# Filler projections of a hybrid encoder layer: split float32r products, streamed rows, all 17 tiles in the delta-net stage

## The chip, the cores and the metric

The kernel runs on one core of one Trainium2 chip. The metric is the device time of one execution in microseconds (us). All data is float32. Some matmul operands are of type float32r, a reduced form of float32 that TensorE takes in a single instruction, where a float32 product of this kernel appears in the trace as two.

## The reference, cut to what matters

One layer of a streaming encoder over 2048 prompt rows, 16 meta rows and 32 sample rows of width 1024. Every row is normed and projected, three groups of heads mix the rows, and the gated result is projected back:

```
u = rmsnorm(h, g_pre) @ W_in          # split into q/k/v of A, B, C, decay inputs, and the gate z
o_A = sliding-window attention with sinks(q_a, k_a, v_a)      # 8 heads, 2 kv heads
o_B = stick-breaking attention(q_b, k_b, v_b)                 # 4 heads
o_C = gated delta net(conv + silu of q/k/v, decay, beta)      # 4 heads, chunks of 64
y = h + rmsnorm((o_A | o_B | o_C) * silu(z) @ W_out, g_post)
```

The outputs are y, the keys and values of A and B, and the conv and delta-net states of C.

## The kernel before, in words

The rows are laid out as T = 2176 columns in 17 tiles of 128 (48 columns of padding, 16 meta rows, 2048 prompt rows, 32 sample rows, padding), and in five blocks `BLOCKS` of 512, 512, 512, 512 and 128 columns. The kernel is a chain of six stages. Each is a block in which every engine has its own program, written out by hand in order, and the engines meet by semaphores alone; a stage ends when all engines are done. SP issues nearly all DMA transfers, in program order.

- `norm_and_transpose` (from L137). Each tile of x is loaded, normed (ACT, DVE), turned by TensorE (L283) and kept in `hT`, a resident buffer of 8 x T columns (L235). The row projections (values and decay inputs) are three products of operands split in two: high part `h_hi` by ACT (L211), low part `h_lo` by DVE (L245), then high x high, high x low, low x high (L294, 392 columns).
- `conv_and_gates`. Six channel tiles as float32 products from `hT` (L463), the conv, SiLU, norms.
- `delta_net` (from L631). Iterations m = 0 to 17. Iteration m inverts a triangle for tile m in five levels and runs the state update for tile m - 1. The products are small (64 columns) and each waits for DVE, ACT or POOL, so TensorE is given filler work between them: 17 projection tiles (5 pairs and singles for q/k, stored to `uT`; 8 gate tiles z, stored to `sz`), of which this stage holds 13. `SideProjection` (L307 to L376) does them. A unit is one tile by one block; a unit has 8 pieces, one for each 128 rows of W_in. `products` (L323) issues pieces, `keep` (L338, on ACT) copies a unit from `side_acc` to `side_stage`, SP stores it (L370) and loads the weights of the tile after next (L361). The hand-made order is `POINTS` (L679): 29 pieces in each iteration, at 13 points (`beside`, L862).
- `window_attention`. No fillers.
- `stick_breaking` (from L1329). 92 steps over the query tiles and up to 512 keys each. In a step TensorE makes scores for two heads (L1491), ACT two sigmoids (L1565, L1568), DVE two scans, one for each head (L1628), with a weight copy between them (L1648), POOL one product (L1606), TensorE transposes (L1508) and the product with the values (L1522). The last four gate tiles are fillers here, two pieces a step, none in the last 12 steps. They are gated to silu(z) by ACT and DVE (L346, L351). When the last filler is done, SP may load `w_out` into `hT` (L1462), paced by the key copies of the last 12 steps.
- `output`. Per tile, load mixed heads, gates and x; sigmoid and multiply for the first `RAWZ` = 4 gate tiles (ACT L1751, POOL L1820); gate all (DVE L1789); split (L1756, L1793); 48 products of 512 columns (L1740); norm, add, store.

The fillers are float32 products, straight from the resident rows:

```
POINTS = [4, 4] + [2, 2] * 5 + [1]                                                  # L679
t, b = divmod(n, NBLK)                                                              # L326
last = pe.matmul(self.acc[:, n % self.banks, 0:width], wslot[:, t % 2, k, :],
                 hT[:, k, c0:c0 + width], start=(k == 0), stop=(k == KT - 1))       # L333
if s < N: side.products(pe, side_piece(s), side_piece(s + 1) - side_piece(s))       # L1551
```

Of the kernel before, what the change touches and what calls it, by code (L numbers as in the profile page):

```python
# [16 lines left out]
F32 = mybir.dt.float32  # L17
# [6 lines left out]
P = 128  # L24
D = 1024
# [23 lines left out]
RAWZ = 4  # L49
# [43 lines left out]
def stream_layer(nc, io):  # L93
    top = ExitStack()
    with top:
# [19 lines left out]
        hT = sb("hT", [P, KT, T])  # L115
# [3 lines left out]
        wslot = sb("wslot", [P, 2, KT, P], st=mixers)  # L119

        mix, uT, sz = io["mix"], io["uT"], io["sz"]
# [4 lines left out]
        w_in = io["w_in"][0].rearrange("(k p) n -> p k n", p=P)  # L126

# [9 lines left out]
        def norm_and_transpose():  # L137
# [4 lines left out]
            with ExitStack() as st:  # L142
# [6 lines left out]
                h_hi, h_lo = (sb(n, [P, 2, KT, P], F32R, st=st) for n in ("h_hi", "h_lo"))  # L149
# [7 lines left out]
                x_in = [sem(f"x_in{i}", st) for i in range(3)]  # L157
                sq_done, ln_done, rstd_done = (sem(n, st) for n in ("sq_done", "ln_done", "rstd_done"))
                scaled, turned, kept = (sem(n, st) for n in ("scaled", "turned", "kept"))
                xp = io["x_prompt"][0]  # L160
                tile_of = lambda n: (0, LAST)[n] if n < 2 else n - 1
                with nc.Block() as block:
                    @block.sync
                    def _(sp):
# [12 lines left out]
                        for n in range(3, 5):  # L177
                            sp.wait_ge(turned, n - 2)
                            sp.dma_start(xin[:, n % 3, :], xp[CH + P * (n - 2):CH + P * (n - 1), :]).then_inc(x_in[n % 3], 32)
                        with sp.Fori(0, (TILES - 5) // 3) as i:  # L180
                            for u in range(3):
                                sp.wait_ge(turned, 3 * i + (u + 3))
                                sp.dma_start(xin[:, (u + 2) % 3, :],
                                             xp[bass.ds(i * (3 * P) + (CH + P * (u + 3)), P), :]).then_inc(x_in[(u + 2) % 3], 32)
                        sp.dma_start(masks, io["cb"]).then_inc(masks_in, 16)
                        sp.dma_start(cf[:, C_TRI:C_EPS], io["cf"][:, C_TRI:C_EPS]).then_inc(masks_in, 16)

                    @block.gpsimd
                    def _(pool):
                        pool.memset(xin[0:CH, 0, :], 0.0).then_inc(zeroed, 1)  # L190
                        pool.memset(xin[SP0 + NSAMP:P, 1, :], 0.0).then_inc(zeroed, 1)

                    @block.scalar
                    def _(act):
# [12 lines left out]
                        def split_high(n):  # L207
                            act.wait_ge(kept, 2 * (n + 1))
                            if n >= 2:
                                act.wait_ge(row_ready, n - 1)  # L210
                            act.activation(h_hi[:, n % 2], hT[:, :, tile_of(n) * P:(tile_of(n) + 1) * P], ACT.Copy).then_inc(high, 1)  # L211
# [15 lines left out]
                    def _(dve):  # L227
# [4 lines left out]
                        def keep(n, slot, cols):  # L232
                            dve.wait_ge(turned, n + 1)
                            for k in (0, KT // 2):
                                dve.tensor_tensor(hT[:, k:k + KT // 2, cols], tp[:, slot, k:k + KT // 2, :],  # L235
# [7 lines left out]
                        def split_low(n):  # L243
                            dve.wait_ge(high, n + 1)
                            dve.tensor_tensor(h_lo[:, n % 2], hT[:, :, tile_of(n) * P:(tile_of(n) + 1) * P], h_hi[:, n % 2].bitcast(F32),  # L245
                                              ALU.subtract).then_inc(low, 1)
# [30 lines left out]
                    def _(pe):  # L277
# [8 lines left out]
                        def row(n):  # L286
                            pe.wait_ge(low, n + 1)
                            if n >= 2:
                                pe.wait_ge(row_kept, n - 1)
                            for k in range(KT):  # L290
                                if n == 0 and k % (KT // 2) == 0:
                                    pe.wait_ge(wv_low, 1 + k // (KT // 2))
                                for p, (h_, w_) in enumerate(((h_hi, wv_hi), (h_hi, wv_lo), (h_lo, wv_hi))):
                                    last = pe.matmul(acc[:, n % 2, 0:RV], h_[:, n % 2, k, :], w_[:, k // 4, k % 4, :],  # L294
# [12 lines left out]
        class SideProjection:  # L307
# [3 lines left out]


            def __init__(self, st, kind, tiles, banks=2):
                self.kind, self.tiles, self.banks = kind, tiles, banks
                self.units = NBLK * len(tiles)
                self.pieces = KT * self.units
                self.stage = sb("side_stage", [P, 2, 512], st=st)
                self.acc = pb("side_acc", [P, banks, 512], st)
# [1585 lines left out]
```

## Time and profile before

| | |
|---|---|
| three runs | 1812.44, 1813.41, 1820.65 us, median 1813.41 |
| profiled execution | 1818.64 us, span of its instructions 1817.0 us |
| mean granted TensorE clock | 0.957 of full speed |
| busy | TensorE 1664.2 us (92%), DVE 893.9, ACT 660.2, POOL 411.8 |
| DMA | 120893 packets, 108.11 MB, 59 GB/s over the span |

Engines: PE is TensorE's matmul, PEld its weight load (which can overlap a matmul), DVE VectorE, ACT ScalarE, POOL GpSimd, SP the queue that issues most DMA transfers. A row of the timeline has its start, its duration (of the union, if it merges several), engine, line, operation, output<-inputs, shape and count, and in brackets the idle time before it with what ended it. Matmul ends are modelled, so the pitch from start to start tells more than a duration. A row of busy time by stretch has the stretch (us from the span's start), its length, the busy us and (x instructions) of PE, PEld, DVE, ACT and POOL, the granted clock, the DMA engines' share and GB/s. The stages begin at about 0, 112, 348, 960, 1162 and 1590 us of the span.

### The profile page before, as it was taken

The page shows a single profiled execution, that of the slowest core. Times are in us where ns is not written, and L with a number is a line of the kernel's source. Part 1 is how long each engine was busy: PE and PEld are TensorE (multiplying, and loading weights), DVE is VectorE, ACT ScalarE, POOL GpSimd, SP SyncE. Part 2 cuts the span into 40 slices and gives each one's busy share as a digit, 9 for nine tenths or more (in the row PEclk, how much of TensorE's full clock was granted, in tenths as well). Part 3 has the DMA queues.
Part 4 walks back from the last instruction along what each step waited for, and adds up shares of the span by engine and source line. Part 5 has one row for each costly group of instructions (what it writes and reads, how often), then busy time and mean ns, then how long its engine had stood idle before and what let it go on. Part 6 is the DMA issues. An engine that isn't in the chain of part 4 may idle for free. (4 is left out here: it accounts for less than half of the span.)

```text
span 1817.0 us, 27973 instructions
## 1 busy us (share of the span) xinstructions
PE 1664.2 (92%) x11144; PEld 998.9 (55%) x11144; DVE 893.9 (49%) x1662; ACT 660.2 (36%) x1321; POOL 411.8 (23%) x344
## 2 busy tenths in 40 slices
PE   5989998299999999999998999799999998769996
PEld 5964444155555555555554555445555555557775
DVE  5724333123333333333334777478687778843332
ACT  4522536011111111111113444345454455456654
POOL 0002321111211211211200000034333434424443
PEclk8999999599999999999996999899999999879998
DMA  4310011411111211112101111100210001466661
GB/s 134 117 26 23 12 63 0 25 37 38 37 38 37 66 38 65 49 37 63 47 31 59 34 60 47 38 30 20 76 32 18 20 18 36 125 172 179 190 182 60
DMA packets 120893, 108.11 MB, mean 59 GB/s; under 512 B 34336, under 2 KB 96064, under 8 KB 120768
## 3 DMA queue, kind: packets, MB, share of 16 engines
q1 hardware_dynamic: 117616, 95.46, 19.2%
q0 software_dynamic: 3152, 10.91, 1.6%
q8 instruction: 87, 1.43, 0.3%
q14 instruction: 38, 0.31, 0.1%
HBM read 65.37 MB, written 41.08 MB: 59 GB/s over the span
## 5 line engine op out<-in xcount | busy, mean ns | idle before, releaser
L333 PE MATMUL side_acc<-hT,wslot 128*128 128x512 f32 (+1 forms) x1360 | 572.8, 550 | 10.1 <-DVE side_stage L351 6.4
L333 PEld LDWEIGHTS side_acc<-hT,wslot 128*128 128x128 f32 x1360 | 223.7, 191 | 178.9 <-issue 155.2
L1628 DVE TENSOR_TENSOR_SCAN prod<-keepb,prod 128x512 f32<-128x512 f32 (+4 forms) x184 | 270.9, 1473 | 86.5 <-ACT keepb L1565 84.1
L1606 POOL TENSOR_TENSOR reg<-reg,prod 128x1024 f32<-128x1024 f32 (+4 forms) x92 | 158.0, 1717 | 465.9 <-DVE prod L1628 465.9
L463 PE MATMUL acc<-hT,wslot 128*128 128x512 f32 (+1 forms) x480 | 180.7, 533 | 5.3 <-DMA wslot<-in_w_in 5.3
L1565 ACT ACTIVATE keepb<-b_z 128x1024 f32<-128x1024 f32 (+4 forms) x92 | 82.0, 891 | 197.2 <-PE b_z L1496 129.2
L463 PEld LDWEIGHTS acc<-hT,wslot 128*128 128x128 f32 x480 | 84.7, 192 | 98.5 <-issue 92.9
L977 DVE COPY yh<-b_two 128x256 f32<-128x256 f32 x85 | 36.1, 424 | 190.9 <-PE b_two L794 190.9
L1740 PE MATMUL b_y<-whi,mhi 128*128 128x512 f32 x272 | 108.3, 398 | 23.1 <-DVE mlo L1793 23.1
L907 ACT ACTIVATE xh<-b_dr 128x256 f32<-128x256 f32 x85 | 32.6, 383 | 211.3 <-PE b_dr L786 211.1
L1740 PE MATMUL b_y<-wlo,mhi 128*128 128x512 f32 x272 | 107.6, 395 | 0.0
L1740 PE MATMUL b_y<-whi,mlo 128*128 128x512 f32 x272 | 107.5, 395 | 0.0
L1508 PE MATMUL b_w<-cf,reg 128*128 128x128 f32 (+1 forms) x624 | 90.0, 278 | 18.2 <-DVE wt L1648 15.0
L728 POOL TENSOR_TENSOR atl<-at,cf 128x256 f32<-128x256 f32 x102 | 72.5, 748 | 126.1 <-DVE at L958 126.1
L1522 PEld LDWEIGHTS b_o<-wt,vrow 128*64 128x64 f32 x1232 | 67.4, 139 | 53.5 <-ACT wt L1583 31.9
L1491 PE MATMUL b_z<-reg 64*128 64x512 f32 (+3 forms) x360 | 90.7, 581 | 4.8 <-PEq L1852 4.8
L733 POOL TENSOR_TENSOR osq<-oo,ors 128x256 f32<-128x256 f32 x17 | 10.4, 613 | 368.9 <-ACT ors L938 368.9
L1508 PEld LDWEIGHTS b_w<-cf,reg 128*128 128x128 f32 (+1 forms) x624 | 66.2, 141 | 47.9 <-DVE wt L1648 19.7
L344 ACT ACTIVATE side_stage<-side_acc 128x512 f32<-128x512 f32 (+1 forms) x65 | 34.6, 532 | 158.9 <-PE side_acc L333 158.9
L1522 PE MATMUL b_o<-wt,vrow 128*64 128x128 f32 x1232 | 89.5, 284 | 2.1 <-DVE reg L1635 2.0
L1568 ACT ACTIVATE reg<-b_z 128x1024 f32<-128x1024 f32 (+4 forms) x92 | 81.3, 884 | 0.0
L1828 POOL TENSOR_TENSOR yy<-yy,xres 128x1024 f32<-128x1024 f32 (+2 forms) x17 | 54.0, 3177 | 106.8 <-DVE yy L1797 94.1
(200 smaller groups left out, 2477.1 us busy)
## 6 DMA issues: line engine op xcount, KB each, us to landing
uT_scratch<-side_stage SPq DMA_DIRECT2D x36, 256.0 KB, 2.0
hT<-mix_scratch SPq DMA_DIRECT2D x17, 512.0 KB, 6.9
hT<-sz_scratch SPq DMA_DIRECT2D x17, 512.0 KB, 8.1
sz_scratch<-side_stage SPq DMA_DIRECT2D x32, 256.0 KB, 2.0
reg<-in_x_prompt SPq DMA_DIRECT2D x15, 512.0 KB
wslot<-in_w_in SPq DMA_DIRECT2D x15, 512.0 KB, 3.9
xres<-in_x_prompt SPq DMA_DIRECT2D x15, 512.0 KB
out_y_prompt<-yy POOLq DMA_DIRECT2D x15, 512.0 KB, 6.4
```

The source lines that it names most:

```text
L333: last = pe.matmul(self.acc[:, n % self.banks, 0:width], wslot[:, t % 2, k, :], hT[:, k, c0:c0 + width], start=(k == 0), stop=(k == KT - 1))
L463: last = pe.matmul(acc[:, b, 0:w], wslot[:, c % 2, k, :], hT[:, k, c0:c0 + w], start=(k == 0), stop=(k == KT - 1))
L728: pool.tensor_tensor(atl[:, l], at[:, :, :], wide(lvl(l), 4), ALU.mult).then_inc(level, 1)
L1491: last = pe.matmul(b_z[0:R, s % 2, hh, 0:nk], reg[half, QS + a, q0:q0 + R], reg[half, KS + a, k0:k0 + nk], start=True, stop=not masks, ski ...
L1508: last = pe.transpose(b_w[0:kn, hh, t, 0:R], beta[0:R, s % 3, hh, at:at + kn], ident[0:R, 0:R])
L1522: last = pe.matmul(b_o[hh * CH:hh * CH + CH, 0:R], v, wt[part, s % 2, hh, t, 0:R], start=(first and t == 0), stop=(last_ and t == len(head ...
L1565: act.activation(keepb[0:R, s % 2, :, 0:nk], b_z[0:R, s % 2, :, 0:nk], ACT.Sigmoid, scale=-SCALE).then_inc(keep_ready, 1)
L1568: act.activation(beta[0:R, s % 3, :, 0:nk], b_z[0:R, s % 2, :, 0:nk], ACT.Sigmoid, scale=SCALE).then_inc(beta_ready, 1)
L1606: pool.tensor_tensor(w, w, prod[0:R, :, c:c + nk], ALU.mult).then_inc(w_ready, 1)
L1628: dve.tensor_tensor_scan(prod[0:R, hh, c0:c0 + nk][:, ::-1], kv, kv, prod[0:R, hh, c0 + nk:c0 + nk + 1], ALU.mult, ALU.bypass).then_inc(pr ...
L1740: last = pe.matmul(b_y[:, s, cols], m_[:, s, k, :], w_[:, k, cols], start=(k == 0 and p == 0), stop=(k == KT - 1 and p == 2))
L1828: pool.tensor_tensor(yy[part, s], yy[part, s], xres[part, s, :], ALU.add).then_inc(summed, 1)
```

## The change

The 17 filler tiles all run in the delta-net stage. Each piece is three float32r products (weight high x row high, low x high, high x low) over six blocks of 350 columns (`SW`), without the padding columns. The rows are no longer resident: the norm stage stores the high and low parts of each tile to a DRAM scratch `hs`, and POOL loads them back, one block (high and low, 8 x 350 columns each) into one of two buffers, a step at a time. A step is one block for a group of tiles; the groups are 5, 4, 4 and 4 tiles, so there are 24 steps. The weights of a group stay in `side_w`, split by ACT and DVE: five splits in iteration 0, which has no fillers now, and 12 after units that free their slot. The padding columns of `uT` and `sz` are zeroed at the end of the norm stage. All gate tiles are stored raw, so `output` gates eight. `hT` is divided into `base`, which later holds the delta-net's small buffers, the raw weights and then w_out, and `upper`, which is freed after the conv stage.

```diff
-RAWZ = 4
+SW = 350
+SBLOCKS = [(PAD + SW * b, min(SW, SROW + NSAMP - PAD - SW * b)) for b in range(...)]
+NSB = len(SBLOCKS)
+RAWZ = KT
...
# norm_and_transpose, SP
+                        def store_split(n):
+                            tok = slice(tile_of(n) * P, (tile_of(n) + 1) * P)
+                            sp.wait_ge(low, 2 * n + 2)
+                            sp.dma_start(hs[0, :, :, tok].rearrange("k p t -> p k t"), h_hi[:, n % 3].bitcast(F32)).then_inc(high_out[n % 3], 16)
+                            sp.dma_start(hs[1, :, :, tok].rearrange("k p t -> p k t"), h_lo[:, n % 2].bitcast(F32)).then_inc(low_out[n % 2], 16)
+                        for n in range(3, TILES):
                             sp.wait_ge(turned, n - 2)
                             sp.dma_start(xin[:, n % 3, :], ...)
+                            store_split(n - 3)
                         sp.dma_start(masks, io["cb"]).then_inc(masks_in, 16)
...
+                        for n in range(TILES - 3, TILES):
+                            store_split(n)
+                        sp.wait_ge(zero_ready, 1)
+                        for scratch, tiles in ((uT, 9), (sz, KT)):
+                            for c0, w in ((0, PAD), (SROW + NSAMP, T - SROW - NSAMP)):
+                                sp.dma_start(scratch[:, :, c0:c0 + w]..., zeros[:, 0:tiles, 0:w]).then_inc(zero_out, 16)
# norm_and_transpose, ACT (split_low on DVE likewise, in two halves, with a wait for low_out)
-                            act.activation(h_hi[:, n % 2], hT[...], ACT.Copy).then_inc(high, 1)
+                            if n >= 3:
+                                act.wait_ge(row_ready, n - 2)
+                                act.wait_ge(high_out[n % 3], 16 * (n // 3))
+                            for k in (0, KT // 2):
+                                act.activation(h_hi[:, n % 3, k:k + KT // 2], rows_of(k, tile_of(n)), ACT.Copy).then_inc(high, 1)
# SideProjection.products
+                    t, b, step = self.order[n]
                     if k == 0:
+                        pe.wait_ge(self.rows_in[step % 2], 32 * (step // 2 + 1))
                         if b == 0:
-                            pe.wait_ge(self.w_in_slot[t % 2], 32 * (t // 2 + 1))
+                            pe.wait_ge(self.w_low, t + 1)
...
+                    for i, (w_part, row_part) in enumerate(((0, 0), (1, 0), (0, 1))):
+                        last = pe.matmul(self.acc[:, n % 2, 0:width], w[:, w_part, k, :], rows[:, row_part, k, 0:width],
+                                         start=(k == 0 and i == 0), stop=(k == KT - 1 and i == 2))
# SideProjection, new
+            def split_high(self, act, t):
+                act.wait_ge(self.w_in_slot[t % 2], 32 * (t // 2 + 1))
+                act.activation(self.w[:, self.slot[t], 0], self.raw[:, t % 2], ACT.Copy).then_inc(self.w_high, 1)
+            def split_low(self, dve, t):
+                dve.wait_ge(self.w_high, t + 1)
+                dve.tensor_tensor(w[:, 1], self.raw[:, t % 2], w[:, 0].bitcast(F32), ALU.subtract).then_inc(self.w_low, 1)
+            def load_rows(self, pool, step):
+                c0, width = SBLOCKS[step % NSB]
+                if step >= 2:
+                    pool.wait_ge(self.acc_ready, self.step_end[step - 2])
+                for a in range(2):
+                    pool.dma_start(self.rows[:, step % 2, a, :, 0:width], hs[a, :, :, c0:c0 + width]...).then_inc(self.rows_in[step % 2], 16)
# SideProjection.transfers: a weight load waits for a split (w_low, t - 1), the first seven are issued at the start
# delta_net
+                side = SideProjection(st, side_tiles, (5, 4, 4, 4), carve(2, KT, P))
-                POINTS = [4, 4] + [2, 2] * 5 + [1]
+                POINTS = [8, 8] + [4, 2] * 5 + [2]
+                PER = sum(POINTS)
+                FIRST = [[(m - 1) * PER + sum(POINTS[:p]) for p in range(len(POINTS))] for m in range(TILES + 1)]
# delta_net, POOL: load_rows(0) and (1) at the start; in iteration m, after the triangle gates
+                            for step in steps_done(m, range(0, 7)):
+                                side.load_rows(pool, step + 2)
# ... and after the output scaling
+                            for step in steps_done(m, range(7, len(POINTS))):
+                                side.load_rows(pool, step + 2)
# stick_breaking: no SideProjection; the keys turn through b_k and krow; SP swaps blocks 3 and 4 at once, then
-                        sp.wait_ge(side.acc_ready, side.units)
-                                side.products(pe, side_piece(s), side_piece(s + 1) - side_piece(s))
# at the end
-            stage(delta_net, cx, [... qk_tiles ...] + z_tiles[0:RAWZ])
+            stage(delta_net, cx, [... qk_tiles ...] + z_tiles)
```

## Rows read from the trace of the kernel before

**Rows 1.** Busy time by stretch: delta-net and stick-breaking stages.
```profile
348.00:960.00 612.00, 598.73 (x5715) 330.27 (x5715) 205.06 (x646) 103.20 (x287) 112.06 (x158) 0.99 0.15 45
...
1162.00:1590.00 428.00, 393.39 (x2746) 224.09 (x2746) 327.79 (x371) 209.62 (x308) 161.51 (x97) 0.97 0.14 43
```
**Rows 2.** Timeline of PE: decay products of iterations 0 to 3, last output transpose.
```profile
350.45 1.06 PE L757 MATMUL b_dr<-tg,cf 128*128 128x256 f32 x2
...
389.58 0.60 PE L757 MATMUL b_dr<-tg,cf 128*128 128x256 f32 x2
...
422.39 0.60 PE L757 MATMUL b_dr<-tg,cf 128*128 128x256 f32 x2
...
454.67 0.60 PE L757 MATMUL b_dr<-tg,cf 128*128 128x256 f32 x2
...
956.02 0.69 PE L858 MATMUL b_s<-cf,oo 128*128 128x128 f32 x2 [2.35 <-POOL oo L740]
```
**Rows 3.** Timeline of PEld inside a burst of wide fillers, first and last of six.
```profile
700.15 0.19 PEld L333 LDWEIGHTS side_acc<-hT,wslot 128*128 128x128 f32 x1 [0.24 <-issue]
...
702.29 0.19 PEld L333 LDWEIGHTS side_acc<-hT,wslot 128*128 128x128 f32 x1 [0.24 <-issue]
```
**Rows 4.** Stick-breaking stage: timeline of POOL, DVE and PE, and the scans' line.
```profile
1165.36 0.64 POOL L1606 TENSOR_TENSOR reg<-reg,prod 128x256 f32<-128x256 f32 x1 [207.03 <-DVE prod L1628]
...
1169.65 3.78 PE L333 MATMUL side_acc<-hT,wslot 128*128 128x512 f32 x4 [0.68 <-DMA wslot<-in_w_in]
...
1175.15 0.86 DVE L1628 TENSOR_TENSOR_SCAN prod<-keepb,prod 128x128 f32<-128x128 f32 x2 [5.44 <-ACT keepb L1565]
...
1503.75 2.00 POOL L1606 TENSOR_TENSOR reg<-reg,prod 128x1024 f32<-128x1024 f32 x1 [2.94 <-DVE prod L1628]
1508.68 2.00 POOL L1606 TENSOR_TENSOR reg<-reg,prod 128x1024 f32<-128x1024 f32 x1 [2.93 <-DVE prod L1628]
...
1566.42 2.00 POOL L1606 TENSOR_TENSOR reg<-reg,prod 128x1024 f32<-128x1024 f32 x1 [2.53 <-DVE prod L1628]
1571.35 2.00 POOL L1606 TENSOR_TENSOR reg<-reg,prod 128x1024 f32<-128x1024 f32 x1 [2.93 <-DVE prod L1628]
...
L1628 DVE TENSOR_TENSOR_SCAN prod<-keepb,prod x184: 456/1275/3070, 1164.4 to 1583.0; 128x512 f32<-128x512 f32 x128, 128x128 f32<-128x128 f32 x20, 128x256 f32<-128x256 f32 x16, 128x384 f32<-128x384 f32 x16
```
**Rows 5.** Timeline of PE: split products of 512 columns (output) and of 392 (norm stage).
```profile
1650.11 0.39 PE L1740 MATMUL b_y<-wlo,mhi 128*128 128x512 f32 x1
...
1651.24 0.39 PE L1740 MATMUL b_y<-whi,mhi 128*128 128x512 f32 x1
...
72.39 0.34 PE L294 MATMUL acc<-wv_lo,h_hi 128*128 128x392 f32 x1
...
76.13 0.34 PE L294 MATMUL acc<-wv_lo,h_hi 128*128 128x392 f32 x1
```
**Rows 6.** Timeline at the start of the delta-net stage: SP's weight loads, the first fillers.
```profile
348.31 4.38 SPq L361 DMA_DIRECT2D wslot<-in_w_in  x4
...
355.54 5.22 PE L333 MATMUL side_acc<-hT,wslot 128*128 128x512 f32 x8 [2.96 <-DMA wslot<-in_w_in]
```
**Rows 7.** Groups by line: total busy us, mean ns, idle before. A split, a gate multiply.
```profile
L245 DVE TENSOR_TENSOR h_lo<-hT,h_hi 128x1024 fp32r<-128x1024 f32 x17 | 20.8, 1225 | 9.9 <-ACT h_hi L211 9.9
...
L1820 POOL TENSOR_TENSOR hT<-hT,zsig 128x512 f32<-128x512 f32 x17 | 23.7, 1394 | 18.4 <-ACT zsig L1751 18.0
```
**Rows 8.** POOL's transfers by line, ns min/median/max: 256 runs (L1596), 128 runs (L1836).
```profile
L1596 POOL DMA_DIRECT2D mix_scratch<-reg x5: 747/748/777, 1220.0 to 1589.0; - x5
...
L1836 POOL DMA_DIRECT2D out_y_prompt<-yy x15: 572/595/609, 1639.6 to 1800.0; - x15
```
**Rows 9.** Busy time by stretch, columns as in rows 1: norm, end of stick-breaking, output.
```profile
57.00:98.00 41.00, 41.00 (x257) 40.71 (x256) 29.93 (x40) 20.52 (x41) 0.00 (x0) 1.00 0.32 104
...
1520.00:1578.00 58.00, 45.24 (x396) 29.00 (x392) 53.95 (x45) 33.20 (x50) 23.56 (x14) 1.00 0.40 112
1630.00:1750.00 120.00, 115.91 (x508) 94.72 (x507) 43.84 (x32) 76.15 (x97) 53.28 (x31) 1.00 0.63 187
```

More of the change, by code:

```diff
@@ L48 @@
 SWAPPED = 3
-RAWZ = 4
+SW = 350
+SBLOCKS = [(PAD + SW * b, min(SW, SROW + NSAMP - PAD - SW * b)) for b in range(-(-(SROW + NSAMP - PAD) // SW))]
+NSB = len(SBLOCKS)
+RAWZ = KT
 LEVELS = 6
@@ L161, in norm_and_transpose @@
                 tile_of = lambda n: (0, LAST)[n] if n < 2 else n - 1
+                rows_of = lambda k, tile: (cx["upper"] if k else base)[:, :, tile * P:(tile + 1) * P]
                 with nc.Block() as block:
@@ L362, in load @@
                         at += width
-                load(0)
-                load(1)
+                for t in range(self.first_size + 2):
+                    load(t)
                 for n in range(self.units):
-                    t, b = divmod(n, NBLK)
-                    c0, width = BLOCKS[b]
+                    t, b, step = self.order[n]
+                    c0, width = SBLOCKS[b]
                     sp.wait_ge(self.staged, n + 1)
                     sp.dma_start(self.tiles[t][1][:, c0:c0 + width], self.stage[:, n % 2, 0:width]).then_inc(self.stored[n % 2], 16)
-                    if b == NBLK - 1 and t + 2 < len(self.tiles):
-                        load(t + 2)
+                    if n in self.splits_after:
+                        load(self.splits_after[n] + 2)
@@ L719, in _ @@
                         triangle_gates(0)
+                        for step in range(2):
+                            side.load_rows(pool, step)
                         for m in range(TILES + 1):
@@ L912, in keep_beside @@
                             for p in points:
-                                for n in range(FIRST[m][p] // KT, min((FIRST[m][p] + POINTS[p]) // KT, side.units)):
+                                for n in units_at(m, p):
                                     side.keep(act, n)
+                                if m == 0 and 3 <= p < 3 + side.first_size:
+                                    side.split_high(act, p - 3)
                         act.preload_act_table_set(LN_EXP)
@@ L1650, in _ @@
                                 scan(s, 1)
-                                for n in side_units(s):
-                                    side.gate(dve, n)
         def output():
-            MIX0, Z0 = D, D + 3 * P
             with ExitStack() as st:
```

233 lines of the change are left out of this document (135 added, 98 removed).

## The prediction

> **What bounds the kernel now.** I read first the busy time by stage [rows 1]. TensorE is busy 598.7 of 612 us in the delta-net stage, which holds 13 of the 17 filler tiles, and 393 of 428 us in the stick-breaking stage, which holds the other four. These shares say where TensorE works, not what a microsecond of it is worth, so each stage is then read at its own scale.
>
> In the delta-net stage one iteration starts at each decay product. Iteration 2 lasts 454.67 - 422.39 = 32.28 us [rows 2]. It carries 29 filler pieces (58 to 86; a tile is 32 wide ones and 8 narrow ones, so 21 are wide and 8 narrow). A wide piece is two instructions 0.428 us apart ((702.29 - 700.15) / 5) [rows 3], so 0.857 us; a narrow one is a quarter of that by its columns, 0.21 us. That is 18.0 + 1.7 = 19.7 us of fillers and 12.6 us for the rest. **TensorE bounds this stage**, and filler time counts in full there.
>
> In the stick-breaking stage the reader should look at the POOL product that closes each step. Two full steps with fillers beside them start it 1508.68 - 1503.75 = 4.93 us apart; two without any (the last filler ran at 1528) 1571.35 - 1566.42 = 4.93 us apart [rows 4]. The scans explain it: one lasts 1.27 us alone and up to 3.07 us, which is what it comes to when it starts beside POOL's product of 2.00 us. So scan, copy, scan and product run one after another, whatever TensorE does. **VectorE and POOL together bound the full steps**, and the fillers there are nearly free.
>
> **Products.** The new form is 17 tiles x 6 blocks x 8 pieces = 816 pieces of three products of 350 columns (346 in the last block), 2448 instructions. The trace has no such width. Split products of 512 columns start 0.226 us apart ((1651.24 - 1650.11) / 5) and those of 392 columns 0.178 us apart ((76.13 - 72.39) / 21) [rows 5]; that is 0.40 ns a column, so 0.162 us at 350. All fillers cost 2448 x 0.162 = 397 us, where they cost 544 x 0.857 + 136 x 0.21 = 495 us before. But only 416 wide and 104 narrow pieces of those stood in the delta-net stage: 356 + 22 = 378 us. The pitch lies between 0.146 us (350 columns at 2.4 GHz, the upper level, which the granted clock of 0.99 in this stage stands for) and 0.19 us, the duration of a weight load [rows 3], if that load can't hide under a short product. I take 0.162, from the nearest rows.
>
> **Delta-net stage.** An iteration now has 48 pieces: 144 x 0.162 = 23.3 us, plus 12.6 us = 35.9 us, for m = 1 to 16. Before, those 16 took from 389.58 to about 933 (23 us ahead of the last output transpose at 956.02), 543 us [rows 2]; after, 574 us: +31. The last pass had 27 pieces (19 wide, 8 narrow, 18.0 us) and gets 48 (23.3 us): +5. The first pass has no fillers any more. It took 39.1 us; what is left is the chain of five levels, some 3 us each (estimate), and five weight splits that wait for their loads. SP needs 4.38 us to issue four loads, and the first filler started 7.2 us after the first issue, released by the load [rows 6]. Five loads through two buffers, beside 5.7 MB of rows, give 34 us (28 to 39): -5. The 12 later splits cost DVE about 1.23 us each, the price of the norm stage's subtraction of the same shape [rows 7], and ACT about as much; bursts of fillers of 0.97 to 1.9 us cover most of it, and I charge 3 us in all (0 to 15). The copies of the side stage grow from 65 to 102 on an ACT that is busy 103 of 612 us: nothing, while unit and copy alternate. The sum is +34 us.
>
> **Row loads.** POOL issues 48 transfers of 1.4 MB in runs of 1400 B, two a step, over 24 steps of 23.9 us (four tiles) or 29.9 us (five). POOL's own issue takes 0.60 us for 128 runs and 0.75 us for 256 [rows 8]; by that slope 1024 runs take 1.7 us, 3.4 us a step. POOL is busy 112 of 612 us, but its triangle products and the output scaling are queued behind, and level 1 of TensorE waits for the first of them. The cover is some 6 us (16 filler pieces lie ahead of level 1), so 3.4 us hides. A load may start up to 10 us late, when POOL is held by the output scaling. The engines moved 187 GB/s at share 0.63 in the output stage [rows 9], so 2.87 MB need about 10 us. 10 + 3.4 + 10 is just under 23.9 us, so I add 2 us for late rows (0 to 60).
>
> **Norm stage.** TensorE paces it: 257 instructions of 32 a tile in 41 us, 5.1 us a tile, and the DMA share of 0.32 with x alone is 1.6 us a tile [rows 9]. New are two stores of 512 KB a tile in runs of 512 B on SP's queue, with the next load of x behind them. The output stage moves x, y and 1 MB in such runs at share 0.63 of 11.3 us a tile (508 instructions of 48), 7.1 us. So the stores need 7.1 - 3.2 = 3.9 us and the tile 5.5 us: the DMA engines become as tight as TensorE. x has two tiles' time of slack, so I charge 0.3 us x 17 = 5 us. At the end SP stores the last tile, then the zero columns, and waits for all: about 5 us more before the next stage. +10 (0 to 22).
>
> **Stick-breaking stage.** What the fillers cost here is only the time between POOL's end and the next scan. Pairing the 92 scans with the products before them I find 27.0 us in 19 places, the first and longest 1175.15 - 1166.00 = 9.15 us at step 1 [rows 4], where 3.78 us of cold products ran; the rest there is the wait for the key cache, and stays. Some of the others are the chain's own. I take -20 us (-27 to -12). The 20 gate multiplies fell into the same waits, worth nothing more. The loads of w_out still wait for the key copies of the last 12 steps.
>
> **Output stage.** All eight gate tiles are now raw, so the first product waits for a POOL multiply of 2.8 instead of 1.4 us [rows 7] and a longer sigmoid: +2. Later they hide under 11 us of TensorE, except at the few tiles where loads are late: +2. Together +4 (+1 to +8). The conv and window stages don't change.
>
> **Sum.** 10 + 34 + 2 - 20 + 4 = +30 us; the profiled execution took 1818.6 us (span 1817.0), so 1848.6. The median of the runs is 5.2 us below it, so I predict **1843 us**.
>
> **Rivals.**
> Rows late (18%): POOL's issue of 1024 runs costs 5 rather than 1.7 us. Some twelve of the 24 steps end late in an iteration, and 10 us then stand ahead of the level products with 6 us of cover: +48 us, 1891. Against it stands only the slope of two rows; for it, that no transfer of such a shape is in the trace. The Trainium skill, SBUF — State Buffer (SBUF: two separate sides), says that transfers issued by GpSimd stall while DVE holds the port that both share; by that rule it would be worse, and the scan of 3.07 us agrees that there is such a lock.
> Stage free (10%): the other side. If the 4.93 us were left over from TensorE's lag after all, the stick-breaking stage would lose its whole filler time, 128 x 0.857 + 32 x 0.21 = 116 us instead of 20, and the total would be 1747. It decides the sign once a full step closes in under 4.46 us, where (4.93 - 4.46) x 64 = 30 us more pay back the rest of the sum. The pitch without fillers speaks against it. A mild form, each term at its good end, gives 25 - 27 + 1 = -1 us, 1812.
> Weight load as floor (5%): 2448 x (0.19 - 0.162) = +69, 1912. The 392-column products start every 0.178 us, below 0.19, which speaks against it.
> Clock falls (4%): without fillers TensorE idles more in the stick-breaking stage. It was busy 78% of the stretch 1520 to 1578, mostly without fillers, at a granted clock of 1.00 [rows 9], so 3.8 us of a full step; at 1.2 GHz up to 7.7 us, and a third of the excess over 4.93 in 64 steps is +60, 1903. The Trainium skill, TensorE: Matmul & The Clock Gate (Part 1), says that a TensorE which idles drops to half rate; that rule would hit the short first rows, and the stretch shows that it spares the full ones.
> The other 63% is my forecast with its bounds.
>
> **Numbers.** Faster 0.12: the stage set free, and a tail. Same, within 0.5% (9 us, about what a measurement of this kernel can tell): 0.13, the mild form. Slower 0.75. The range 1808 to 1891 leaves out about two in ten.
>
> **What would show it.** Right: filler products 0.16 us apart, iterations of 36 us without waits, full steps still 4.93 us, a stick-breaking stage of 408 us, a first pass of 34 us. Wrong: products idle for POOL or for the rows (rows late), a pitch near 0.19 (weight loads), full steps near 4 us (stage free), a norm tile well over 5.5 us (stores dearer than loads in such runs).

## The result, and the profile after

The kernel after takes 1839.5 us (median of 4 runs, 1838.6 to 1845.3), beside 1817.0 us before (median of 4 runs, 1812.4 to 1821.5). The ratio is 1.013 with a 95% interval of 1.009 to 1.017. The change costs about 22 us, 1.3%. The profiled execution has a span of 1837.7 us against 1817.0 us, 20.7 us more, and the accounts below are made against that.

The busy time of the whole execution, from the page of the kernel after:

```profile
span 1837.7 us, 30393 instructions
PE 1597.0 (87%) x12232; PEld 1183.8 (64%) x12232; DVE 961.7 (52%) x1676; ACT 684.9 (37%) x1372; POOL 474.4 (26%) x393
```

A stage is counted here from its first TensorE instruction to that of the next stage (the last one to the end of the span), from the traces of both kernels:

| stage | before | after | difference | predicted |
|---|---|---|---|---|
| norm | 106.6 | 109.2 | +2.6 | +10 |
| conv | 234.0 | 237.7 | +3.7 | 0 |
| delta net | 610.9 | 648.6 | +37.7 | +36 |
| window attention | 201.3 | 196.5 | -4.8 | 0 |
| stick-breaking | 443.1 | 419.8 | -23.3 | -20 |
| output | 211.4 | 216.2 | +4.8 | +4 |
| lead-in, the same | 9.7 | 9.7 | 0 | |
| sum | 1817.0 | 1837.7 | +20.7 | +30 |

Three stretches of the kernel after, in windows like those of [rows 1] and [rows 9] (length, then busy time and instructions of each engine, granted clock, DMA share, GB/s):

```profile
57.00:98.00 41.00, 41.00 (x256) 40.70 (x255) 29.01 (x48) 21.37 (x48) 0.00 (x0) 1.00 1.01 303
354.00:1000.00 646.00, 614.58 (x7123) 550.45 (x7123) 228.84 (x663) 128.15 (x341) 153.47 (x203) 0.96 0.61 159
1201.00:1604.00 403.00, 312.34 (x2426) 188.24 (x2426) 371.73 (x351) 199.54 (x288) 161.32 (x97) 0.91 0.10 30
```

In the norm stage the DMA share has gone from 0.32 to 1.01, and TensorE still issues 256 instructions in 41 us, where it issued 257 [rows 9]. In the delta-net stage TensorE is busy 614.6 of 646 us. In the stick-breaking stage it is busy 312 of 403 us, while VectorE is at 372 of 403: with the fillers gone, the stage lost only 23 us, a fifth of the 116 us of TensorE time that they had taken.

The delta-net stage in the timeline of TensorE (start, length, instructions merged). The first line of a pair of decay products opens a pass, as in [rows 2]:

```profile
356.77 1.06 PE L843 MATMUL b_dr<-base,cf 128*128 128x256 f32 x2
395.63 1.06 PE L843 MATMUL b_dr<-base,cf 128*128 128x256 f32 x2
433.18 0.60 PE L843 MATMUL b_dr<-base,cf 128*128 128x256 f32 x2
439.46 6.03 PE L385 MATMUL side_acc<-side_rows,side_w 128*128 128x350 f32 x36
468.76 0.60 PE L843 MATMUL b_dr<-base,cf 128*128 128x256 f32 x2
```

The pass without fillers (its pair comes first) takes 395.63 - 356.77 = 38.9 us, a pass with 48 pieces 468.76 - 433.18 = 35.6 us; 15 of the 16 passes between decay products lie at 35.6 to 37.5 us, and none has a wait for rows. In the burst of 36 products, whose last one takes 0.32 us, they start (6.03 - 0.32) / 35 = 0.163 us apart; the median distance over all 2448 is 0.161 us.

The row loads, all on one line of POOL (count, then shortest, median and longest time of POOL's own issue in ns, first and last start; below, from issue to landing):

```profile
L415 POOL DMA_DIRECT2D side_rows<-hs_scratch x48: 880/900/953, 356.5 to 956.9; - x48
DMA to landing us min/median/max: 6.9/10.7/14.9
```

And POOL's products in full steps of the stick-breaking stage, to be set beside [rows 4]:

```profile
1532.32 2.00 POOL L1688 TENSOR_TENSOR reg<-reg,prod 128x1024 f32<-128x1024 f32 x1 [2.93 <-DVE prod L1710]
1537.26 2.00 POOL L1688 TENSOR_TENSOR reg<-reg,prod 128x1024 f32<-128x1024 f32 x1 [2.93 <-DVE prod L1710]
1542.19 2.00 POOL L1688 TENSOR_TENSOR reg<-reg,prod 128x1024 f32<-128x1024 f32 x1 [2.93 <-DVE prod L1710]
```

They stand 4.93 us apart, the number of before to the last digit. Of the 43 distances between two full steps 27 are 4.93 us, before as after, and the other 16 are shorter (4.53 to 4.80 us). Two of the distances of 4.93 us after lie wholly at the lower level of TensorE's clock, of which this is one:

```profile
1413.79 2.00 POOL L1688 TENSOR_TENSOR reg<-reg,prod 128x1024 f32<-128x1024 f32 x1 [2.53 <-DVE prod L1710]
1418.72 2.00 POOL L1688 TENSOR_TENSOR reg<-reg,prod 128x1024 f32<-128x1024 f32 x1 [2.93 <-DVE prod L1710]
```

```profile
1413.79:1418.72 4.93, 4.08 (x20) 2.56 (x22) 4.88 (x6) 1.26 (x3) 2.00 (x2) 0.50 0.00 0
```

At a granted clock of 0.50 it still takes 4.93 us, with VectorE busy for 4.88 of them. No two such steps follow each other in this trace.

### The profile page after: what moved, and what is told of

Same layout as the page of the kernel before. It is cut to its first block and busy times, and to the rows that moved or that the text cites. A ratio compares the mean times of both kernels' runs of the same rounds, so it can differ in the third digit from the quotient of the medians.

```text
span 1837.7 us, 30393 instructions
## 1 busy us (share of the span) xinstructions
PE 1597.0 (87%) x12232; PEld 1183.8 (64%) x12232; DVE 961.7 (52%) x1676; ACT 684.9 (37%) x1372; POOL 474.4 (26%) x393
## 5 line engine op out<-in xcount | busy, mean ns | idle before, releaser
L385 PE MATMUL side_acc<-side_rows,side_w 128*128 128x350 f32 (+1 forms) x2448 | 447.0, 332 | 0.0
L385 PEld LDWEIGHTS side_acc<-side_rows,side_w 128*128 128x128 f32 x2448 | 389.2, 189 | 15.3 <-issue 2.9
L1710 DVE TENSOR_TENSOR_SCAN prod<-keepb,prod 128x512 f32<-128x512 f32 (+4 forms) x184 | 326.2, 1774 | 19.6 <-ACT keepb L1651 15.5
L404 ACT ACTIVATE side_stage<-side_acc 128x350 f32<-128x350 f32 (+1 forms) x102 | 47.1, 462 | 285.8 <-PE side_acc L385 285.8
L1066 DVE COPY base<-b_two 128x256 f32<-128x256 f32 x85 | 36.1, 424 | 217.1 <-PE b_two L880 217.1
L530 PE MATMUL acc<-base,wslot 128*128 128x512 f32 (+1 forms) x240 | 95.1, 540 | 7.6 <-DMA wslot<-in_w_in 7.6
L1611 PEld LDWEIGHTS b_o<-wt,vrow 128*64 128x64 f32 x1232 | 74.7, 150 | 39.3 <-issue 19.4
L810 POOL TENSOR_TENSOR base<-base,cf 128x256 f32<-128x256 f32 x102 | 71.6, 739 | 86.1 <-DVE base L1047 86.1
L530 PE MATMUL acc<-upper,wslot 128*128 128x512 f32 (+1 forms) x240 | 92.6, 529 | 0.0
L415 POOL DMA_DIRECT2D side_rows<-hs_scratch x48 | 43.4, 907 | 150.4 <-PE side_acc L385 150.4
L994 ACT ACTIVATE base<-b_dr 128x256 f32<-128x256 f32 x85 | 32.5, 382 | 130.3 <-PE b_dr L872 130.3
```

Source lines behind the costliest of these rows:

```text
L385: last = pe.matmul(self.acc[:, n % 2, 0:width], w[:, w_part, k, :], rows[:, row_part, k, 0:width], start=(k == 0 and i == 0), stop=(k == K ...
L404: act.activation(self.stage[:, n % 2, 0:width], self.acc[:, n % 2, 0:width], ACT.Copy).then_inc(self.staged, 1)
L530: last = pe.matmul(acc[:, b, 0:w], wslot[:, c % 2, k, :], hT(cx, k)[:, c0:c0 + w], start=(k == 0), stop=(k == KT - 1))
L810: pool.tensor_tensor(atl[:, l], at[:, :, :], wide(lvl(l), 4), ALU.mult).then_inc(level, 1)
L1611: last = pe.matmul(b_o[hh * CH:hh * CH + CH, 0:R], v, wt[part, s % 2, hh, t, 0:R], start=(first and t == 0), stop=(last_ and t == len(head ...
L1710: dve.tensor_tensor_scan(prod[0:R, hh, c0:c0 + nk][:, ::-1], kv, kv, prod[0:R, hh, c0 + nk:c0 + nk + 1], ALU.mult, ALU.bypass).then_inc(pr ...
```

## The experiments

Lines of this section are those of each experiment's own kernel, a few off from those above. Stages are counted as in the table. Edits are cut to what matters ("..."); without another word they are made to the kernel after. The experiments ran on three chips, on which the kernel before took 1809.9, 1810.5 and 1811.0 us (medians of 7 runs), so a total is best set beside these, and a stage beside the stages above.

### What the gating of twenty units and the eight raw tiles are worth: before_raw_gates

The edit is made to the kernel before. ACT copies a unit in place of a sigmoid, and the multiply of VectorE is left out.

```
-    RAWZ = 4
+    RAWZ = KT
-    side = SideProjection(st, "silu", side_tiles, banks=1)
+    side = SideProjection(st, "copy", side_tiles, banks=1)
-                                for n in side_units(s):
-                                    side.gate(dve, n)
```

> The kernel before, but the last four gate tiles are stored raw (a copy, no sigmoid and no multiply by VectorE in the stick-breaking stage) and the output stage gates all eight. Theory: the stick-breaking stage keeps its 426 us within 2 us, since the 20 multiplies fell into waits for TensorE, and the output stage grows by 3 to 6 us as it did in the kernel after; total +2 to +5 us. Rival (the multiplies of 0.7 us stood in VectorE's chain): stick-breaking stage -14 us, total -9 us.

It took 1812.7 us (one run) beside a median of 1809.9 us for the kernel before on that chip. Its stick-breaking stage took 434.2 us instead of 443.1, and its output stage 219.7 us instead of 211.4. So the total came out as the theory had it (a single run can't tell 3 us from nothing, as the seven runs of before lie between 1807.5 and 1818.1), and both of its parts were wrong: the gating was worth 9 us, not nothing, and eight raw tiles cost 8 us, not 3 to 6. The 9 us fall on eight of the 92 steps, 0.3 to 2.4 us each. One such step, in the timeline of VectorE, first of the kernel before, in which the multiply of the last narrow unit (L351) runs at 1436.36:

```profile
1436.36 0.26 DVE L351 TENSOR_TENSOR side_stage<-side_acc,side_stage 128x128 f32<-128x128 f32 x1
1443.65 1.28 DVE L1628 TENSOR_TENSOR_SCAN prod<-keepb,prod 128x512 f32<-128x512 f32 x1 [3.35 <-ACT keepb L1565]
```

and then the same step with a copy by ACT in its place:

```profile
1428.69 1.60 DVE L1628 TENSOR_TENSOR_SCAN prod<-keepb,prod 128x512 f32<-128x512 f32 x1 [0.66 <-ACT keepb L1565]
```

The multiply lasts 0.26 us, and the wait of the scan is 2.7 us longer with it. It is the step that frees the single accumulator of the fillers, and it stands behind a scan on VectorE. TensorE can't begin the next unit before it, and the scores of the next step are queued behind the fillers on TensorE. That this is the way of the delay is read from the order on the queues, not shown by itself; the sigmoid, which went with the multiply, was not tried alone.

### What the fillers cost in the stick-breaking stage: tail_tiles_in_stick

The products of the last four gate tiles go back into the stick-breaking stage in the new form. Their rows are streamed there too, in eight blocks of 262 columns. For the space, the buffer of the lower half rows is given up ahead of that stage, and the rows, later W_out, take its place.

```
-    POINTS = [8, 8] + [4, 2] * 5 + [2]
+    POINTS = [6, 6] + [3, 2] * 5 + [1]
-    side = SideProjection(st, side_tiles, (5, 4, 4, 4), carve(2, KT, P))
+    side = SideProjection(st, side_tiles, (5, 4, 4), carve(2, KT, P))
...
+    side = SideProjection(st, side_tiles, (2, 2), side_raw, TBLOCKS, side_rows, krow, b_k)
+    QUIET = N - TAIL - 2 * side.units
+    def side_piece(s):
+        return KT // 2 * max(0, min(s, N - TAIL) - QUIET)
...
+    side.products(pe, side_piece(s), side_piece(s + 1) - side_piece(s))
```

> Theory (TensorE bounds the delta-net stage, VectorE and POOL together the stick-breaking stage, so filler products are dear in the first and nearly free in the second): 13 tiles stay in the delta-net stage with 38 pieces a pass instead of 48. An iteration falls from 35.6 by 30 x 0.161 = 4.8 to 30.8 us, the stage by about 85 us. The last four tiles run in the stick-breaking stage as 256 pieces of three 262-column products (768 x 0.121 = 93 us of TensorE), where full steps must stay at 4.93 us and the stage grows by 15 to 25 us over the 403 us that it has without them. Total about 1775 us. Rival 1 (POOL's issue of the rows stands in the closed chain of scans and products): 14 steps of rows x 1.8 us and four splits of 1.2 us on VectorE come on top, +30 us, 1805. Rival 2 (fillers are only cheap there because TensorE was idle at the cold start): full steps grow to 5.3 us, +24 us, 1800.

It took 1760.6 us (median of 4 runs), a ratio of 0.971 (0.968 to 0.975) to the kernel before: **2.9% faster than before, and by the two ratios (0.971 to 1.013) some 4% faster than the kernel after.** Ten of the passes take 30.7 to 30.8 us, and the delta-net stage 559.1 us, 89.5 less than after. The stick-breaking stage takes 424.5 us, where the five kernels without any filler there take 419.8 to 422.2. So 93 us of TensorE time cost 2 to 5 us there, not the expected 15 to 25. The output stage takes 222.7 us, 6.5 more than after, which was not expected: all kernels with fillers in the stick-breaking stage and eight raw tiles take 219.7 to 223.2 us in it, those without such fillers 215.0 to 217.3; why was not tested. Full steps stay at 4.93 us (26 of 43, one is 5.83 us, the rest are the shorter ones of above), and TensorE is busy 60.6 of 63 us in a stretch of them:

```profile
1400.00:1463.00 63.00, 60.63 (x532) 44.83 (x532) 61.91 (x47) 33.45 (x49) 29.05 (x18) 1.00 0.40 86
```

Neither rival holds. POOL issues the rows right behind its product, while VectorE scans:

```profile
1372.21 1.09 POOL L1728 TENSOR_TENSOR reg<-reg,prod 128x512 f32<-128x512 f32 x1 [1.86 <-DVE prod L1753]
1373.26 1.82 POOL L420 DMA_DIRECT2D side_rows<-hs_scratch  x2
1376.25 1.99 POOL L1728 TENSOR_TENSOR reg<-reg,prod 128x1024 f32<-128x1024 f32 x1 [1.17 <-DVE prod L1753]
```

The issue fits into the time for which POOL waits for the scans, with 1.17 us to spare.

### The first pass: rows1_later

```
-                        for step in range(2):
-                            side.load_rows(pool, step)
+                        side.load_rows(pool, 0)
...
+                            if m == 0:
+                                pool.wait_ge(side.w_low, 5)
+                                side.load_rows(pool, 1)
```

> Theory (the first pass of the delta-net stage is long because five weight loads share the DMA engines with 5.7 MB of rows): the second block of rows is asked for only when the fifth weight is split, so 2.8 MB less stand beside the weights; the first pass falls from 38.9 to 31 to 34 us, the rest stays, total -5 to -7 us. Rival (the weights wait for their two buffers, one load after the other, and not for the engines): the first pass stays within 1 us of 38.9.

The first pass took 30.2 us instead of 38.9, the second 38.2 instead of 37.5, the delta-net stage 640.6 instead of 648.6, and the total was 1830.8 us (one run). ACT's copy of the third weight shows why; first the kernel after, then this one:

```profile
382.66 1.06 ACT L392 ACTIVATE side_w<-base 128x1024 fp32r<-128x1024 f32 x1 [11.21 <-DMA base<-in_w_in]
```

```profile
370.13 1.06 ACT L392 ACTIVATE side_w<-base 128x1024 fp32r<-128x1024 f32 x1 [3.61 <-DMA base<-in_w_in]
```

The stage's first decay products are at 356.8 us in the first and some 4 us earlier in the second, so the weight is in 8 us sooner. The weights had been sharing the DMA engines with rows whose first product comes only at 427.5 us in the kernel after, 45 us behind that split. The first pass gains 8.7 us, more than the expected 5 to 8, and the second gives 0.6 back.

### Is TensorE the bound in every pass: two_products

```
-    for i, (w_part, row_part) in enumerate(((0, 0), (1, 0), (0, 1))):
+    for i, (w_part, row_part) in enumerate(((0, 0), (0, 1))):
...
```

> Left out: the product of the weights' low part with the rows' high part. Theory (TensorE bounds every iteration of the delta-net stage, and its products stand 0.161 us apart): 816 fewer, an iteration falls by 48 x 0.161 = 7.7 us to 27.9 us, the stage by 16 x 7.7 + 5 = 128 us, total 1711. Rival (the chain of levels is close behind): an iteration can't go below some 30 us, total 1745.

It took 1712.4 us (one run), with most passes (11 of 16) at 28.0 to 28.2 us. This kernel leaves out the weights' low part, which the result needs, so its time is no version's time:

```profile
705.77 0.60 PE L843 MATMUL b_dr<-base,cf 128*128 128x256 f32 x2
733.86 0.60 PE L843 MATMUL b_dr<-base,cf 128*128 128x256 f32 x2
```

The theory's 27.9 us holds; the chain of levels is still not the bound. With the commonest passes of the other runs this makes a straight line to within 0.2 us, 12.6 us + 0.161 us a product: 96 products 28.1 us, 105 products 29.5, 114 products 31.0, 144 products 35.8, where 28.1, 29.5, 30.8 and 35.6 us were measured.

### The price of the stores: double_stores

```
     sp.dma_start(hs[0, ...], h_hi[:, n % 3]...).then_inc(high_out[n % 3], 16)
     sp.dma_start(hs[1, ...], h_lo[:, n % 2]...).then_inc(low_out[n % 2], 16)
+    sp.dma_start(hs2[0, ...], h_hi[:, n % 3]...).then_inc(high_out[n % 3], 16)
+    sp.dma_start(hs2[1, ...], h_lo[:, n % 2]...).then_inc(low_out[n % 2], 16)
...     # the waits for high_out and low_out count twice as far
```

> The kernel after, with the two stores of each tile in the norm stage made twice (the second pair to a scratch tensor that nobody reads). Theory (a DMA share of 1.01 means that the 16 engines are full, and the tile of 5.1 us hides the stores only just): the stores' packet time of 3.5 us a tile comes on top, a tile takes 8.5 us, the stage +55 to +60 us, total 1895. Rival (the share adds up the times of packets that wait beside each other, so it is no measure of a full engine): tiles stay under 5.6 us, total within 8 us of 1838.

It took 1885.6 us (one run), and its norm stage 161.0 us, 52 more than after. Any nine tiles in a row in its middle took 74.5 to 76.4 us, some 8.4 us each. That is the theory's tile of 8.5 us, with a stage and a total a little under the expected ones. In the same stretch as above:

```profile
57.00:98.00 41.00, 30.89 (x154) 29.88 (x155) 18.58 (x30) 13.17 (x30) 0.00 (x0) 0.83 1.06 314
```

The share rises from 1.01 to 1.06 and no further, the rate from 303 to 314 GB/s, while TensorE falls to 154 instructions. The kernel after is thus at the edge in this stage: its stores are hidden, and one more of that size would not be, by an estimate (half of the two stores' 3.6 us of packets a tile is 0.35 of share, where 0.05 is left). One more alone was not tried.

### How much cover POOL has: pool_busier

```
+                for _ in range(3):
+                    pool.wait_ge(self.spared, self.spares)
+                    self.spares += 1
+                    pool.tensor_tensor(self.spare, self.other, self.other, ALU.mult).then_inc(self.spared, 1)
```

> The kernel after, with three multiplies of 128x256 behind each issue of rows on POOL (some 0.7 us each, so POOL holds 3.9 instead of 1.8 us a step of rows). Theory (about 6 us of fillers cover what stands on POOL ahead of the level products): nothing changes, passes stay at 35.6 to 36.2 us, total within 3 us of 1838. Rival (POOL's level products have little slack, and the issue was cheap only because it took 0.9 instead of 5 us): passes with such a step grow by 1 to 2 us, total +20 to +45 us.

It took 1838.2 us (one run), and passes 3 to 16 have the lengths of the kernel after to within 0.02 us. The three multiplies took 2.01 us behind an issue of 1.81 us, so work on POOL of somewhat more than the issue's own length is hidden; longer work wasn't tried.

### More tiles in the stick-breaking stage: six, four and five

six_in_stick gives the stage six tiles, 16 pieces in every three steps; the delta-net stage keeps eleven, and asks for the second block of rows late:

```
+    QUIET = N - TAIL - 3 * side.units // 2
...
+    return 2 * KT * (q // 3) + (0, KT, KT + KT // 2)[q % 3]       # q: steps since QUIET
```

> Eleven tiles in the delta-net stage (32 pieces a pass), six in the stick-breaking stage (384 pieces, 16 in every three steps), and the second block of rows asked for late as in rows1_later. Theory: an iteration of the delta-net stage falls to the 28.1 us at which the run with two products stopped, since TensorE's own need would be 26.2 us and the chain of levels takes over, so that stage loses 16 x 2.7 = 43 us and 7 to 9 us in its first pass. In a full step of the stick-breaking stage TensorE needs 3.1 us at full clock without fillers and 16/3 x 3 x 0.121 = 1.94 us with them, 5.04 us against the 4.93 us of VectorE and POOL: the stage grows by 5 to 15 us over the run with four tiles there. Total 1720 us (1712 to 1732). Rival (a step that carries a whole unit, 2.9 us of products, delays its scans, because scores stand only one step ahead): 24 such steps x 1.1 us more, and POOL's issue of 24 blocks of rows, +35 to 45 us in that stage, total 1745 to 1755.

It took 1752.8 us (median of 5 runs; ratio to before 0.967, 0.965 to 0.970), not the theory's 1720. The delta-net stage lost what was expected (511.0 us). My reason for the 28.0 us of a pass was wrong: by the line above it is TensorE's own 12.6 + 96 x 0.161 = 28.1 us, and no floor. The rival was right on the other stage: 472.3 us, 48 more than with four tiles. Beside the kernel after, 33 steps are more than 0.3 us longer, 52 us in all, and 28 of them carry a whole unit or stand right behind one. The stage also has 10 us of TensorE's waits for rows, in a line below; how its growth divides between bursts, total load and these waits is not shown.

four_in_stick_rows_later puts tail_tiles_in_stick and rows1_later together:

> tail_tiles_in_stick with the second block of rows asked for late, as in rows1_later. Theory (the two edits add up, since one shortens the first pass and the other every later one): total 1760.6 - 7 = 1753 us. Rival (a pass is now 4.8 us shorter and needs that block sooner, so the gain is given back as a wait in the second pass): 1759 to 1761 us.

It took 1747.8 us (median of 4 runs), a ratio of 0.966 (0.962 to 0.969). The two edits add up (first pass 30.1 us, 7.3 less; the second 0.6 more, the others unchanged). **This is the lowest median that was found, 3.4% below the kernel before**, but six_in_stick, at 0.967 (0.965 to 0.970), can't be told from it. Some 4.3 us of its distance to tail_tiles_in_stick are the window stage (196.7 against 201.0 us), which the edit doesn't touch.

five_in_stick_rows_later was to spread the load, with a whole unit only in every ninth step, and tiles in groups of two, two and one (lines taken out are those of six_in_stick):

```
...
-    side = SideProjection(st, side_tiles, (2, 2, 2), side_raw, TBLOCKS, side_rows, krow, b_k)
+    side = SideProjection(st, side_tiles, (2, 2, 1), side_raw, TBLOCKS, side_rows, krow, b_k)
...
+    return 5 * KT * (q // 9) + (KT // 2 * (q % 9 + 1) if q % 9 else 0)
```

> Twelve tiles in the delta-net stage (35 pieces a pass), five in the stick-breaking stage: 40 units in 72 steps, only every ninth step carries a whole unit, all others half a unit as with four tiles. Theory (the 47 us that six tiles cost there came from the steps with a whole unit, 24 of them, some 1.9 us each): 8 such steps cost 15 us and the longer occupation 3 us, while the passes fall from 30.8 to the floor of 28.1 to 28.3 us, -41 us. Total 1753 - 41 + 18 = 1730 us (1722 to 1740). Rival (TensorE's total load decides, not the bursts): half of the 47 us comes with the fifth tile, and the total is 1735 to 1745 us.

A miss for both: 1787.5 us (median of 4 runs, 1780.3 to 1791.6). Passes took 29.5 us, as the line above says and I had not worked out, and the stick-breaking stage 478.8 us. TensorE's waits in that stage (engine, line, releaser, sum, times, longest), of five tiles and then of six:

```profile
PE b_k L390 <- DMA side_rows<-hs_scratch: 35.6, 10, 7.6
```

```profile
PE b_k L390 <- DMA side_rows<-hs_scratch: 9.9, 10, 2.3
```

and of five tiles, two steps late in the stage:

```profile
1420.94 1.81 POOL L420 DMA_DIRECT2D side_rows<-hs_scratch  x2
1430.46 5.61 PE L390 MATMUL b_k<-side_rows,side_w 128*128 128x262 f32 x24 [5.80 <-DMA side_rows<-hs_scratch]
```

Here the rows are late at last. The likely reason: the single tile of the last group needs a new block for every unit, two steps or 9.9 us apart, while POOL's issue, the landing and the wait for the buffer take as long; a group of two tiles needs one in twice that time. The waits for rows come to 36 us in a stage that is 54 us longer than with four tiles. So this run says nothing on bursts against total load: whether five tiles in a better order would beat four stays open.

## Why the prediction was right, point by point

The predicted 1843 us stands against 1839.5, inside the range, and the sign is the predicted one. The difference was met less well than the total: +30 us predicted, +20.7 measured in the spans. The 1843 stood on a median of 1813.4 us for the kernel before; with the 1817.0 of its four runs, +30 would have meant 1847. That both lie so close is in part luck, and the errors are in the steps:

**What bounds each stage** was right, and carries the result. In the delta-net stage every product counts: 144, 114, 105 and 96 products a pass lie on one line. In the stick-breaking stage full steps are 4.93 us with four tiles of fillers, with none, and with four in the other form. "Stage free" is out. "Clock falls" had its condition right and its price wrong: the granted clock of the stage went from 0.97 to 0.91, and full steps kept their 4.93 us, one of them wholly at 0.50, where up to 7.7 us had been reckoned.

**Pitch.** 0.162 us was taken from two widths in [rows 5]; the median is 0.161 us, and 262 columns give 0.122 us (median distance in tail_tiles_in_stick), 0.46 to 0.47 ns a column at either width. "Weight load as floor" is out: the loads still last 0.19 us [rows 3], now as well, and hide.

**Iterations.** 35.9 us predicted, 35.6 measured; three of them take 36.0 to 36.2 us, and the first 37.5 us, which is where splits and the first rows fall. That is 3 to 4 us in all, where 3 were charged. All 16 take 572.8 us against 540.4 before, +32.4, where 31 + 3 were predicted. The 543 us for before were 3 us too many: the transposes that open its last pass start at 929.69, not near 933.

**First pass.** Predicted -5 us, measured -0.3 (38.9 against 39.1 us). The step that failed is "five loads through two buffers, beside 5.7 MB of rows, give 34 us": the sharing of the DMA engines was named and priced too low, by 5 us. rows1_later shows that it was this sharing.

**Last pass.** Predicted +5 us. From the output transposes that open it to the last one it takes 31.4 us (968.09 to 999.49) against 26.3 us before (929.69 to 956.02), +5.1.

**Row loads.** POOL's issue was put at 1.7 us for 1024 runs and is 0.90 us. The slope from 128 to 256 runs does not go on: 0.60, 0.75 and 0.90 us for 128, 256 and 1024. No product waited for rows, so +2 became 0, and "Rows late" did not come. pool_busier shows that even 3.9 us a step are hidden, so the 3.4 us that the sum reckoned with would have been; the 10 us of the rival were not tried. The Trainium skill, SBUF — State Buffer (SBUF: two separate sides), says that transfers issued by GpSimd stall while DVE holds the shared port, and names for it an operation of DVE in a mode that uses two ports. The row speaks against a stall of that kind beside the scans here: in tail_tiles_in_stick POOL issues rows in a stage in which VectorE is busy 88% of the time (373 of 425 us), twelve of the issues lie wholly inside a scan, and no issue of the run takes longer than 0.96 us:

```profile
L420 POOL DMA_DIRECT2D side_rows<-hs_scratch x68: 881/900/956, 351.9 to 1430.9; - x68
```

**Norm stage.** Predicted +10, measured +2.6. Two terms were too large. The tiles stay at 5.17 us, since 3.6 us of packets a tile (1.01 x 5.17, less 1.6 for x) just fit beside the loads of x, and TensorE shows no slowing beside them (256 instructions in 41 us, 257 before). 3.9 us had been taken from the output stage, whose runs of 512 B are loads. And the end costs 2.4 us, not 5. double_stores confirms the mechanism: the stage is a few per cent of share from being bound by DMA.

**Stick-breaking stage.** Predicted -20 (-27 to -12), measured -23.3. The step that failed is "the 20 gate multiplies fell into the same waits, worth nothing more": before_raw_gates puts the gating at 9 us of the 23. The fillers' products were worth the rest, 12 to 14 us (434.2 us against 419.8 to 422.2 in the five kernels without fillers), less than the 20 that I had given them. Two errors cancel, and that the term came out so close is luck.

**Output stage.** +4 predicted, +4.8 measured; 8 us in before_raw_gates, and between 4 and 12 us in the others. The 8 us with fillers ahead and the 5 us without say that eight raw tiles cost more than +4, and that a stick-breaking stage without fillers gives some back, a term that the sum had at nothing; the second is read from the stages and has no test of its own.

**What no step foresaw.** +3.7 us in the conv stage and -4.8 in the window stage, which the change doesn't touch. From the last conv product to the first of the delta-net stage VectorE and ACT end early and SP waits for small stores; that gap is 41.0 us before, 44.1 after, and 38.1 to 41.5 in the nine others. It is scatter. The window stage takes 196.5 to 197.5 us in seven of the eleven traces and 200.9 to 201.3 in the other four, before among the latter. The difference lies in its first 30 us, in which products of one shape take either 1.03 or 0.62 us; first before, 28 us into the stage, then after, 19 us into it:

```profile
989.05 1.03 PE L1178 MATMUL b_sc<-cb 128*128 128x512 bf16 x2
```

```profile
1024.57 0.62 PE L1280 MATMUL b_sc<-cb 128*128 128x512 bf16 x2
```

TensorE had been idle for about 5 us ahead of that stage in both and came back to the upper level of its clock at different times: the granted clock is 0.50 in the first 28.7 us of the stage before and in the first 19.4 us after, and 1.00 right behind. In the other nine traces it returns 28.7 to 29.0 us into the stage where the stage is long, and 19.7 to 21.5 us where it is short. These two terms together are -1 us, so they don't touch the sign, but each is as large as some steps of the sum.

**The sum.** Against their predictions the norm stage came out 7.4 us lower, the rows 2.0 and the stick-breaking stage 3.3 lower, the delta-net stage 3.7 and the output stage 0.8 higher, and the two untouched stages 1.1 lower together. That makes the 9.3 us by which +30 was too high.

## What to carry to other kernels

Work that fills gaps of an engine must be put where another engine is the bound: four tiles' products, 93 us of TensorE, cost 90 us in one stage and 2 to 5 us in the other, and making them cheaper (three reduced products for one float32 product) only pays where they count. Look for the share of each stage, and then for the pitch of its repeating step with and without the fillers. When prefetches are added, ask what is loading at the same moment and is needed first: a block of rows that was needed 45 us later held up the weights that could not.

## What was unexpected in the hardware

A share of DMA time of 1.01 still hid everything, and twice the stores brought it to 1.06 and 314 GB/s, with tiles at 8.4 instead of 5.2 us: in this stage a share near 1.0 is the edge itself. POOL's issue of a transfer in 1024 runs takes 0.90 us, hardly more than one in 256 runs (0.75 us), and doesn't grow beside a busy VectorE. A full step of the stick-breaking stage took its 4.93 us even with TensorE at half clock. And a stage that is not touched can move by 4 to 5 us, by the moment at which TensorE's clock returns to its upper level.
